# Expert rows: gathered and summed at the end, or scaled and added into the residual in DRAM as they are made

## The chip, the cores and the metric

One core of one Trainium2 chip runs the whole program. The metric is device time in microseconds for one execution, taken as a median of unprofiled runs: 1065.59 us for the kernel before (three runs, 1063.46 to 1066.72). A separate, profiled execution gives the trace.

## The reference

A two-layer decoder trunk over 512 tokens of width 1024, in float32. Layer 0 is latent attention and a dense SwiGLU; layer 1 is a pooling mixer and a routed mixture of experts; a last RMSNorm follows. What matters here is the end of layer 1:

```python
hn = rms_norm(h, ffn_norm[1])
# each token: its top 2 of 8 experts by hn @ router, gates = softmax of the two logits
y[token] = gate0 * expert0(hn[token]) + gate1 * expert1(hn[token])
# expert(x) = (silu(x @ w_gate) * (x @ w_up)) @ w_down, inner width 1344
h = h + y
out = rms_norm(h, final_norm)
```

## The kernel before

The tokens sit in `h`, four tiles (t = 0 to 3) of 128 tokens by 1024. After the router, the 1024 (token, expert) pairs are sorted into *jobs*, each one expert and a block of rows; job j owns rows j*144 on of two DRAM buffers, `xbuf` (normed inputs) and `ybuf` (expert outputs). GpSimd scatters the normed tokens into `xbuf` with eight indirect DMAs (L738; the row numbers are `dest`). With this input there are two *wide* jobs (144 rows, plain float32 matmuls, L1594 and L1618), then five *narrow* jobs in a loop and a *final* narrow job (128 rows). `before_last`, `narrow` and the expert of each job are read from a table at run time.

A narrow job needs its expert's 16.5 MB of weights. SP loads them as 18 units u0 to u17 of about 1 MB (two DMAs each, u17 half as large) into nine raw buffers (`RAWS`); it issues unit u when the unit nine earlier has been used (`n_used`). ScalarE rounds each unit to its high part (`unit_hi`, L1062), VectorE subtracts for the low part (`unit_lo`, L2250), and TensorE multiplies three times (L1190 to L1192). Units 0 to 7 and 10 to 13 are gate and up columns; `silu(f)`, `product(f)` (L2321), `turn(f)` (transposes, L1698), `act_hi_out(f)` (L1128) and `act_lo_out(f)` (L2326) bring activation group f to the down projection, which is `down_pair` over u8, u9, u14 to u17. `down_pair(1, 0)` (u14) waits for `act_lo_out(1)`. ScalarE's order near the end of a job is u13, u14, u15, `act_hi_out(1)`, u16, u17, `silu(2)`. VectorE's is u12, u13, u14, `act_lo_out(1)`, u15, u16, u17, `product(2)`.

At the end of a wide or a looped narrow job ScalarE and VectorE each copy one half of the job's output out of PSUM (L1103 and L2282; L1164 and L2372), and GpSimd stores it to `ybuf` (L753, L763, L775), waits for the landing and frees the buffer. GpSimd also loads the next job's rows from `xbuf` (L743, L749, L760, L772).

The final job's output is never stored. The tokens in it, and enough others to fill 128, are called *slots*. While the final job runs, GpSimd gathers, two per tile, the rows of `ybuf` that belong to tiles 0 to 2 (L782, `y_rows`), then three tiles for the slots (L791: their residual from `hbuf` and up to two rows of `ybuf`), and, once tile 0 is summed, the two of tile 3. VectorE adds them with their gates (`add_y`, L2302, two instructions per tile, put between the `unit_lo` of u12 to u15; `add_slots`, L2312). ScalarE squares (L1172) and VectorE scales (L2383) each tile after the final job's own work, SP stores the four tiles. Last, the slots' rows take the final job's PSUM (L2392), are normed (L1176 to L2398) and scattered over the output once the four stores have landed (L798).

`hbuf` holds a copy of the residual, stored by SP (`keep_h`) before the first job. During the dense feed-forward, GpSimd writes zeros to all of `xbuf` (L723) and to the rows of `ybuf` that no job may write (L727, L730).

Of the kernel before, what the change touches and what calls it, by code (L numbers as in the profile page):

```python
# [24 lines left out]
F32 = mybir.dt.float32  # L25
# [7 lines left out]
P = 128  # L33
# [34 lines left out]
YPIECES = 2 * (FI - 2)  # L68
YZERO = -(-(JMAX - E) * C // YPIECES)
# [84 lines left out]
def trunk(nc, a, out):  # L154
    plan = plan_weights()
    with ExitStack() as ctx:
# [49 lines left out]
        from_y = sb("from_y", [P, 2 * T], I32)  # L206
        gate_y = sb("gate_y", [P, 2 * T])
        spare_b = sb("spare_b", [P, T], BF16)
        slot_vals = sb("slot_vals", [P, T, 8])
        slot_info = sb("slot_info", [P, 8])  # L210
        slot_at = sb("slot_at", [P, 4], I32)
# [72 lines left out]
        y_in = view(0, 6 * D, 6)  # L284
        slot_h, slot_a, slot_b = (view((6 + n) * D, D) for n in range(3))
        slot_y = y_in[:, 2, :]
        n_x = view(4096, D)

# [34 lines left out]
        ybuf = nc.dram_tensor("ybuf", (JMAX * C, D), F32, kind="Internal").ap()  # L323
        hbuf = nc.dram_tensor("hbuf", (S, D), F32, kind="Internal").ap()
# [17 lines left out]
        y_gathered = [sem(f"y_gathered{t}") for t in range(T)]  # L342
# [114 lines left out]
        h_final = sem("h_final")  # L457
# [181 lines left out]
        def _(pool):  # L639
# [13 lines left out]
            for m in (ident, ident_b):  # L653
# [13 lines left out]
            g.iota(slot_vals[:, :, :], [[P, T], [0, 8]], base=0, channel_multiplier=1, allow_small_or_imprecise_dtypes=True  # L667
                   ).then_inc(iotas_ready, 1)
            g.iota(iota_j[:, :], [[1, NJ]], base=0, channel_multiplier=0, allow_small_or_imprecise_dtypes=True
                   ).then_inc(iotas_ready, 1)  # L670

# [44 lines left out]
            for i in range(FI):  # L716
                for j in range(FG):
                    if j == 0:
                        pool.wait_ge(prod_ready, i * FG + 2)
                    elif j == 2 and i < FI - 1:  # L720
                        pool.wait_ge(h_ffn, i * 8 + 4)
                    at = (i * FG + j) * XZERO
                    pool.dma_start(xbuf[at:at + XZERO, :], zero_rows[0:XZERO, :]).then_inc(zero_stored, 16)  # L723
                if i < E - 1:
                    at = (i + 1) * C + P if i else (E - 1) * C
                    rows = min(C - P if i else P, JMAX * C - YPIECES * YZERO - at)
                    pool.dma_start(ybuf[at:at + rows, :], zero_rows[0:rows, :]).then_inc(zero_stored, 16)  # L727
                for n in range(2 * i, min(2 * i + 2, YPIECES)):
                    at = JMAX * C - (n + 1) * YZERO
                    pool.dma_start(ybuf[at:at + YZERO, :], zero_rows[0:YZERO, :]).then_inc(zero_stored, 16)  # L730
# [5 lines left out]
            pool.wait_ge(zero_stored, 16 * (FI * FG + YPIECES + E - 1))  # L736
# [3 lines left out]
            pool.wait_ge(scattered, 16 * 2 * T)  # L740
            pool.sem_inc(yn_free, 1)
            pool.wait_ge(xT_done, 1)
            pool.dma_start(xg, xbuf[C:2 * C, :].rearrange("(k p) n -> p k n", p=CH)).then_inc(xg_landed, 16)  # L743
            pool.wait_ge(routed, 1)
            before_last = pool.value_load(table[0:1, NJ + 3:NJ + 4], min_val=1, max_val=JMAX - 1)
            with pool.Fori(0, before_last) as job:
# [3 lines left out]
                               ).then_inc(xg_landed, 16)  # L750
                pool.wait_ge(y_ready, job + 2)
                pool.wait_ge(y_ready_dve, job + 2)
                pool.dma_start(ybuf[bass.ds(job * C, C), :].rearrange("(k p) n -> p k n", p=CH), yn  # L753
                               ).then_inc(y_stored, 16)
                pool.wait_ge(xg_landed, job * 16 + 32)
                pool.wait_ge(y_stored, job * 16 + 16)
# [6 lines left out]
            pool.dma_start(ybuf[bass.ds(before_last * C, C), :].rearrange("(k p) n -> p k n", p=CH), yn  # L763
                           ).then_inc(y_stored, 16)
            pool.wait_ge(y_stored, before_last * 16 + 16)
            pool.sem_inc(n_y_free, 1)
            narrow = pool.value_load(table[0:1, NJ + 2:NJ + 3], min_val=1, max_val=JMAX)
            with pool.Fori(0, narrow) as n:

                pool.wait_ge(n_x_turned, n + 1)  # L770
                job = job_of(n + before_last + 1)
                pool.dma_start(n_x, xbuf[bass.ds(job * C + 2 * C, P), :]).then_inc(n_x_landed, 16)  # L772
                pool.wait_ge(n_y_left, n + 2)
                pool.wait_ge(n_y_right, n + 2)
                pool.dma_start(ybuf[bass.ds(job * C, P), :], n_y[:, :]).then_inc(n_y_stored, 16)  # L775
                pool.wait_ge(n_x_landed, n * 16 + 32)
                pool.wait_ge(n_y_stored, n * 16 + 16)
                pool.sem_inc(n_y_free, 1)

            def y_rows(t):  # L780
                for k in range(2):
                    pool.indirect_dma_start(out=y_in[:, (2 * t + k) % 6, :], out_offset=None, in_=ybuf,  # L782
                                            in_offset=bass.IndirectOffsetOnAxis(ap=from_y[:, k * T + t:k * T + t + 1], axis=0)
                                            ).then_inc(y_gathered[t], 16)

            pool.wait_ge(slots_known, 1)
            pool.wait_ge(h_stored, 16 * T)
            for t in range(T - 1):
                y_rows(t)
            for n, (dst, src) in enumerate(((slot_h, hbuf), (slot_a, ybuf), (slot_b, ybuf))):  # L790
                pool.indirect_dma_start(out=dst, out_offset=None, in_=src,  # L791
                                        in_offset=bass.IndirectOffsetOnAxis(ap=slot_at[:, n:n + 1], axis=0)
                                        ).then_inc(slot_landed, 16)
            pool.wait_ge(h_final, 1)
            y_rows(T - 1)
# [7 lines left out]
        def _(act):  # L803
# [224 lines left out]
            act.wait_ge(zero_stored, 16 * (FI * FG + YPIECES + E - 1))  # L1028
# [35 lines left out]
            def expert_job(job, final=False):  # L1064
# [37 lines left out]
                for b in range(2):  # L1102
                    last = s.copy(yn[:, 0, b * 512:b * 512 + 512], bank[4 + b][0:CH, :])  # L1103
# [12 lines left out]
            def narrow_job(n, final=False):  # L1116
# [24 lines left out]
                silu(1)  # L1141
                for u in (13, 14, 15):
                    unit_hi(u, n)
# [3 lines left out]
                if final:  # L1147
                    silu(2)
                    s.activation(warm[:, 0:1], eps_t[:, 0:1], ACT.Sqrt)
                    act_hi_out(2)  # L1150
                    return
# [12 lines left out]
                s.copy(n_y[:, 0:512], bank[4][:, :]).then_inc(n_y_left, 1)  # L1164
# [4 lines left out]

            for t in range(T):  # L1170
                act.wait_ge(h_final, t + 1)
                link(s.activation(n_y[:, :], h[:, t, :], ACT.Square, scale=D ** -0.5, accum_out=sumsq[:, t:t + 1]))  # L1172
                s.activation(rms[:, t:t + 1], sumsq[:, t:t + 1], ACT.Sqrt, bias=eps_t[:, 0:1]).then_inc(std_ready, 1)
# [11 lines left out]
        def _(pe):  # L1185
# [452 lines left out]
            def expert_job(job, final=False):  # L1638
# [16 lines left out]
                else:  # L1655
                    pe.wait_ge(slots_ready, 1)
                    for t in range(T):
                        last = t_.matmul(bank[2][:, 0:6], slot_of[:, t, :], slot_vals[:, t, 0:6], start=t == 0, stop=t == T - 1)
# [98 lines left out]
        def _(dve):  # L1757
# [388 lines left out]
            link(v.tensor_tensor(gate1[:, :], gate1[:, :], gate0[:, :], ALU.mult))  # L2146

# [42 lines left out]
            rel, in_last, out_last, near = (field(2 * n, 2) for n in range(4))  # L2190
            any_last, spare, slot, other = (field(8 + n) for n in range(4))
            at_last, own, moved, bound = (field(12 + n) for n in range(4))
            base_of, top_of, full = bound[:, 0:1], bound[:, 1:2], bound[:, 2:3]
# [227 lines left out]
```

## Time and profile before

| | us |
|---|---|
| median of three unprofiled runs | 1065.59 |
| the profiled execution | 1071.8 |
| its span (first to last instruction) | 1070.1 |
| TensorE busy in the span | 1017.4 |
| VectorE / ScalarE / GpSimd busy | 601.2 / 453.8 / 73.1 |

The mean granted TensorE clock is 0.983 of full speed. 226.55 MB move by DMA, 212 GB/s over the span. In the page's strip of 40 slices, TensorE is at 9 tenths or more in almost all but the last two (6 and 3), and the DMA engines are at 9 tenths in the ten slices before the last two. To read it: a busy engine is only a bound where nobody else makes it wait, and the average over the span says little about one stage. The stages that matter here are routing (604 to 620 us), the wide jobs (621 to 761), the narrow loop (761 to 994), the final job (994 to 1058) and the tail behind it.

### The profile page before, as it was taken

The numbers are of one execution on the slowest core, as the hardware profiler recorded it, in microseconds if no ns is written. First come the engines' busy times: TensorE is split into PE (matmuls) and PEld (weight loads), VectorE is DVE, ScalarE is ACT, GpSimd is POOL, SyncE is SP. The second block draws the span as 40 slices with busy tenths as digits, with TensorE's granted clock in tenths as the row PEclk, the third lists the DMA queues.
The fourth block names the chain that finished last, engine by engine and source line by source line (L and its number), as shares of the span: only waits on it lengthen the run. The fifth ranks groups of instructions, "written<-read, shape, count | busy, mean of one in ns | idle before, by whom it ended". The sixth has DMA issues, their size and how long they took to land.

```text
span 1070.1 us, 15078 instructions
## 1 busy us (share of the span) xinstructions
PE 1017.4 (95%) x5506; PEld 873.6 (82%) x5506; DVE 601.2 (56%) x816; ACT 453.8 (42%) x603; POOL 73.1 (7%) x138
## 2 busy tenths in 40 slices
PE   5999999999999999999999789999999999999963
PEld 5887887788888888888889679999887888888852
DVE  6575666354443434343457630100788989889875
ACT  5535554244232222223144200101777777777633
POOL 2200000000010100000000030000000000000330
PEclk9999999999999999999999899999999999999986
DMA  8021322535373736445327576895999999999982
GB/s 281 2 79 41 128 69 81 136 100 160 130 202 97 218 103 195 137 135 156 100 78 256 197 243 195 270 335 184 372 356 389 364 392 368 368 389 366 391 310 98
DMA packets 150155, 226.55 MB, mean 212 GB/s; under 512 B 16676, under 2 KB 97572, under 8 KB 150112
## 3 DMA queue, kind: packets, MB, share of 16 engines
q1 hardware_dynamic: 138464, 187.98, 52.6%
q0 software_dynamic: 10832, 37.44, 10.0%
q8 instruction: 28, 0.46, 0.2%
q10 hardware_dynamic: 816, 0.54, 0.2%
q14 instruction: 15, 0.12, 0.0%
HBM read 196.92 MB, written 29.02 MB: 211 GB/s over the span
## 4 chain that ended last, share of the span: by engine, by line
PE 86%; DVE 6%; DMA 3%; ACT 2%; issue 2%; SPq 0%; POOLq 0%; DVEq 0%; ACTq 0%
PE bank L1190 22%; PE bank L1191 22%; PE bank L1192 22%; PE bank L1594 8%; PE bank L1618 4%; DMA u_raw<-in_moe_w_down 2%; PE bank L1362 1%; PE bank L1202 1%; PE bank L1573 1%; PE bank L1342 1%; PE bank L1353 1%; PE bank L1499 1%; DVE w_lo L1771 1%; DVE u_lo L2250 1%; PE bank L1698 1%
## 5 line engine op out<-in xcount | busy, mean ns | idle before, releaser
L2250 DVE TENSOR_TENSOR u_lo<-u_raw,u_hi 128x2048 fp32r<-128x2048 f32 (+1 forms) x108 | 217.6, 2046 | 12.2 <-ACT u_hi L1062 11.8
L1062 ACT CAST u_hi<-u_raw 128x2048 fp32r<-128x2048 f32 (+1 forms) x108 | 185.0, 1723 | 73.9 <-DMA u_raw<-in_moe_w_up 37.5
L1190 PE MATMUL bank<-big_hi,w_lo 128*128 128x512 f32 (+2 forms) x352 | 134.4, 382 | 0.0
L1192 PE MATMUL bank<-big_hi,w_hi 128*128 128x512 f32 (+2 forms) x352 | 134.3, 381 | 0.0
L1191 PE MATMUL bank<-big_lo,w_hi 128*128 128x512 f32 (+2 forms) x352 | 134.2, 381 | 0.0
L1771 DVE TENSOR_TENSOR w_lo<-stage_own,w_hi 128x1024 fp32r<-128x1024 f32 (+1 forms) x89 | 103.3, 1207 | 13.8 <-ACT w_hi L817 13.8
L1190 PE MATMUL bank<-u_hi,nx_lo 128*128 128x512 f32 (+1 forms) x288 | 106.5, 370 | 0.0
L1004 ACT ACTIVATE scratch<-bank 128x512 f32<-128x512 f32 x21 | 12.6, 598 | 218.8 <-PE bank L1192 218.8
L1192 PE MATMUL bank<-u_hi,nx_hi 128*128 128x512 f32 (+1 forms) x288 | 104.5, 363 | 0.0
L1191 PE MATMUL bank<-u_lo,nx_hi 128*128 128x512 f32 (+1 forms) x288 | 104.5, 363 | 0.0
L2028 DVE TENSOR_TENSOR scratch<-scratch,bank 128x512 f32<-128x512 f32 x21 | 14.5, 688 | 151.6 <-ACT scratch L1004 151.6
L817 ACT CAST w_hi<-stage_own 128x1024 fp32r<-128x1024 f32 (+1 forms) x89 | 87.0, 1036 | 10.6 <-DMA stage_own<-in_mla_w_uq 5.6
L1594 PE MATMUL bank<-scratch,u_raw 128*128 128x144 f32 x640 | 84.4, 290 | 4.6 <-issue 3.1
L1594 PEld LDWEIGHTS bank<-scratch,u_raw 128*128 128x128 f32 x640 | 81.6, 193 | 5.5 <-issue 3.7
L1190 PE MATMUL bank<-w_hi,act_lo_mem 128*128 128x512 f32 (+1 forms) x216 | 81.5, 377 | 0.6 <-DVE act_lo_mem L1831 0.6
L1191 PE MATMUL bank<-w_lo,act_hi_mem 128*128 128x512 f32 (+1 forms) x216 | 80.7, 373 | 0.0
L1192 PE MATMUL bank<-w_hi,act_hi_mem 128*128 128x512 f32 (+1 forms) x216 | 80.6, 373 | 0.0
L1190 PEld LDWEIGHTS bank<-big_hi,w_lo 128*128 128x128 f32 x352 | 66.1, 188 | 12.8 <-issue 0.2
L1192 PEld LDWEIGHTS bank<-big_hi,w_hi 128*128 128x128 f32 x352 | 66.1, 188 | 12.4
L1191 PEld LDWEIGHTS bank<-big_lo,w_hi 128*128 128x128 f32 x352 | 66.1, 188 | 12.4
L1190 PE MATMUL bank<-u_hi,na_lo 128*128 128x512 f32 (+1 forms) x132 | 55.3, 419 | 8.2 <-DVE na_lo L2326 7.3
L2256 DVE TENSOR_TENSOR qr_now<-krT,bank 128x144 f32<-128x144 f32 x20 | 6.1, 304 | 99.6 <-ACT krT L1070 99.0
(342 smaller groups left out, 1746.9 us busy)
## 6 DMA issues: line engine op xcount, KB each, us to landing
u_raw<-in_moe_w_gate SPq DMA_DIRECT2D x68, 512.0 KB, 6.8
u_raw<-in_moe_w_up SPq DMA_DIRECT2D x68, 512.0 KB, 8.1
u_raw<-in_moe_w_down SPq DMA_DIRECT2D x64, 512.0 KB, 9.5
stage_own<-in_ffn_w_gate SPq DMA_DIRECT2D x21, 512.0 KB, 6.0
stage_own<-in_ffn_w_up SPq DMA_DIRECT2D x21, 512.0 KB, 7.2
stage_own<-in_ffn_w_down SPq DMA_DIRECT2D x21, 512.0 KB, 4.4
xbuf<-scratch POOLq DMA_DIRECT2D x21, 496.0 KB, 5.9
u_raw<-in_moe_w_down SPq DMA_DIRECT2D x8, 1024.0 KB, 7.8
```

What stands on the lines that cost most here:

```text
L817: s.copy(w_hi[0:parts, sl, 0:n], stage(st)[0:parts, 0:n]).then_inc(weight_hi, 1)
L1004: s.activation(f_silu[:, j % 2, :], bank[2 * (j % 2)][:, :], ACT.Silu).then_inc(silu_ready, 1)
L1062: s.copy(u_hi[u % HIS][0:rows, 0:size], u_raw[u % RAWS][0:rows, 0:size]).then_inc(n_hi, 1)
L1190: t_.matmul(dst, st_lo, mv_hi, start=start, stop=False, skip_group_check=check)
L1191: t_.matmul(dst, st_hi, mv_lo, start=False, stop=False, skip_group_check=check)
L1192: return t_.matmul(dst, st_hi, mv_hi, start=False, stop=stop, skip_group_check=check)
L1202: last = t_.transpose(bank[banks[k // 4]][:, k % 4 * P:k % 4 * P + P], src[:, k * P:(k + 1) * P], ident[:, :])
L1594: last = t_.matmul(dst[:, 0:C], u_raw[u % RAWS][:, at:at + P], xT[:, k, :], start=k == 0, stop=k == KD - 1)
L1618: last = t_.matmul(bank[4 + k // 3][:, col:col + C], u_raw[u % RAWS][0:parts, at:at + P], e_act[0:parts, f % 2, :], start=f == 0 and k % 3 ...
L1771: v.tensor_tensor(w_lo[0:parts, sl, 0:n], stage(st)[0:parts, 0:n], w_hi[0:parts, sl, 0:n], ALU.subtract).then_inc(weight_lo, 1)
L2028: v.tensor_tensor(f_act[:, j % 2, :], f_silu[:, j % 2, :], bank[2 * (j % 2) + 1][:, :], ALU.mult).then_inc(prod_ready, 1)
L2250: v.tensor_tensor(u_lo[u % RAWS][0:rows, 0:size], u_raw[u % RAWS][0:rows, 0:size], u_hi[u % HIS][0:rows, 0:size], ALU.subtract).then_inc(n ...
```

## The change

Each job's output row is multiplied by its gate while it leaves PSUM, and the GpSimd DMA that stored it is replaced by an indirect DMA that adds it to its token's row of `hbuf`. For this a small DRAM table `info` holds, per job row, the token number and the gate. It is filled by two strided DMAs with "no token" entries (rows 512 to 655 of `hbuf`, gate zero) and by eight indirect DMAs of 8 bytes per row after those to `xbuf`. Before each addition GpSimd loads the job's part of the table and waits for it. At the end, one gather brings the slots' rows from `hbuf` and four plain loads bring `h` back; ScalarE squares the tiles within the final job.

```diff
+            for c in range(2 * T):
+                pool.indirect_dma_start(out=info, out_offset=bass.IndirectOffsetOnAxis(ap=dest[:, c:c + 1], axis=0),
+                                        in_=token_gate[:, c, :], in_offset=None).then_inc(scattered, 16)
...
             with pool.Fori(0, narrow) as n:
-                pool.wait_ge(n_x_turned, n + 1)
+                pool.wait_ge(n_x_hi, n + 2)
                 pool.dma_start(n_x, xbuf[...]).then_inc(n_x_landed, 16)
+                pool.wait_ge(final_landed, 16)
                 pool.wait_ge(n_y_left, n + 2)
                 pool.wait_ge(n_y_right, n + 2)
-                pool.dma_start(ybuf[bass.ds(job * C, P), :], n_y[:, :]).then_inc(n_y_stored, 16)
+                pool.indirect_dma_start(out=hbuf, out_offset=bass.IndirectOffsetOnAxis(ap=n_info[:, 0:1], axis=0),
+                                        in_=n_y[:, :], in_offset=None, compute_op=ALU.add).then_inc(n_y_stored, 16)
                 pool.wait_ge(n_x_landed, n * 16 + 32)
                 pool.wait_ge(n_y_stored, n * 16 + 16)
+                pool.dma_start(n_info[:, :], info[bass.ds(job * C + C, P), :]).then_inc(n_info_landed, 16)
+                pool.wait_ge(n_info_landed, n * 16 + 32)
                 pool.sem_inc(n_y_free, 1)
...
             pool.wait_ge(slots_known, 1)
-            pool.wait_ge(h_stored, 16 * T)
-            for t in range(T - 1):
-                y_rows(t)
-            for n, (dst, src) in enumerate(((slot_h, hbuf), (slot_a, ybuf), (slot_b, ybuf))):
-                pool.indirect_dma_start(out=dst, ...)
-            pool.wait_ge(h_final, 1)
-            y_rows(T - 1)
+            pool.indirect_dma_start(out=slot_h, out_offset=None, in_=hbuf, ...).then_inc(slot_landed, 16)
+            for t in range(T):
+                pool.dma_start(h[:, t, :], hbuf[t * P:(t + 1) * P, :]).then_inc(h_back, 16)
```

On ScalarE, in the final job, and the scaled copies (VectorE's halves likewise, `tensor_scalar` in place of `tensor_copy`):

```diff
-                    last = s.copy(yn[:, 0, ...], bank[4 + b][0:CH, :])
+                    last = s.activation(yn[:, 0, ...], bank[4 + b][0:CH, :], ACT.Copy, scale=yn_gate[:, 0, :])
...
+                def square(t):
+                    act.wait_ge(h_back, 16 * T)
+                    link(s.activation(n_y[:, :], h[:, t, :], ACT.Square, scale=D ** -0.5, accum_out=sumsq[:, t:t + 1]))
+
+                if final:
+                    for t, u in enumerate((13, 14, 15)):
+                        unit_hi(u, n)
+                        square(t)
+                    act_hi_out(1)
+                    square(3)
+                    unit_hi(16, n)
+                    unit_hi(17, n)
+                    silu(2)
+                    s.activation(rms[:, 0:T], sumsq[:, 0:T], ACT.Sqrt, bias=eps_t[:, 0:1]).then_inc(std_ready, 1)
+                    act_hi_out(2)
+                    return
```

VectorE loses `add_y` and `add_slots`, and most of the small routing instructions of L2217 to L2233, and gains two 128x4 copies into `token_gate` after L2146. The slots' sum takes one value of the matmul of `slot_of` in place of three. `ybuf` and its zeros are gone; two stores of zeros to `hbuf` rows 512 to 655 and the two strided stores to `info` take their place. The same narrow-loop pattern holds in the wide jobs, where the addition is two indirect DMAs of 72 rows.

## Rows read from the trace of the kernel before

**Rows 1.** The page, section 4: shares of the chain that ended last.

```profile
PE 86%; DVE 6%; DMA 3%; ACT 2%; issue 2%; SPq 0%; POOLq 0%; DVEq 0%; ACTq 0%
```

**Rows 2.** Windows: one narrow job, the final job's first 46.5 us, the rest.

```profile
core 0: us, PE busy (x) PEld busy (x) DVE busy (x) ACT busy (x) POOL busy (x), PEclk, DMA share, GB/s
949.40:995.90 46.50, 46.50 (x230) 39.13 (x229) 41.14 (x29) 34.84 (x29) 1.07 (x2) 1.00 1.03 378
995.90:1042.40 46.50, 39.21 (x182) 32.81 (x180) 35.43 (x25) 23.34 (x19) 18.30 (x12) 0.90 0.95 353
1042.40:1070.10 27.70, 10.12 (x33) 7.58 (x33) 16.83 (x22) 10.09 (x23) 0.99 (x1) 0.68 0.24 95
```

**Rows 3.** Windows of 5 us in the final job, the same columns.

```profile
1020.00:1025.00 5.00, 5.00 (x32) 4.64 (x31) 4.56 (x5) 1.64 (x2) 2.74 (x2) 1.00 1.03 409
1025.00:1030.00 5.00, 4.63 (x32) 4.36 (x30) 3.89 (x4) 1.58 (x1) 2.90 (x2) 1.00 1.02 407
1030.00:1035.00 5.00, 0.00 (x0) 0.00 (x0) 2.29 (x1) 1.66 (x2) 0.00 (x0) 0.77 1.05 347
1035.00:1040.00 5.00, 3.10 (x7) 2.51 (x8) 3.88 (x4) 1.05 (x2) 0.00 (x0) 0.50 0.74 220
1040.00:1045.00 5.00, 2.39 (x6) 1.34 (x4) 4.96 (x4) 4.66 (x5) 0.00 (x0) 0.71 0.00 1
```

**Rows 4.** Timeline of PE: start, length, line; final job's first, gated and last instructions.

```profile
994.19 0.50 PE L1190 MATMUL bank<-u_hi,nx_lo 128*128 128x512 f32 x1
...
1036.90 0.79 PE L1190 MATMUL bank<-u_hi,na_lo 128*128 128x512 f32 x1 [7.28 <-DVE na_lo L2326]
...
1047.78 0.69 PE L1698 MATMUL bank<-ident,na_nat 128*128 128x128 f32 x2 [5.39 <-DVE na_nat L2321]
...
1057.51 0.39 PE L1192 MATMUL bank<-u_hi,na_hi 64*128 64x512 f32 x1
```

**Rows 5.** Timeline of ACT: u14, u15, act_hi_out(1) and a square, final job.

```profile
1028.42 1.91 ACT L1062 CAST u_hi<-u_raw 128x2048 fp32r<-128x2048 f32 x1 [3.90 <-DMA u_raw<-in_moe_w_down]
1033.67 1.90 ACT L1062 CAST u_hi<-u_raw 128x2048 fp32r<-128x2048 f32 x1 [3.34 <-DMA u_raw<-in_moe_w_down]
1035.47 0.58 ACT L1128 CAST na_hi<-bank 128x512 fp32r<-128x512 f32 x1
...
1049.15 1.06 ACT L1172 ACTIVATE n_y<-h 128x1024 f32<-128x1024 f32 x1
```

**Rows 6.** Groups of instructions by line: the sums removed and the scatter before routing ends.

```profile
L2302 DVE SCALAR_TENSOR_TENSOR h<-scratch,gate_y,h 128x1024 f32<-128x1024 f32 x8 | 10.2, 1281 | 0.1
L2312 DVE SCALAR_TENSOR_TENSOR scratch<-scratch,slot_info 128x1024 f32<-128x1024 f32 x2 | 2.6, 1278 | 0.0
...
L738 POOL DMA_INDIRECT xbuf<-scratch,dest x8 | 7.8, 976 | 42.6 <-DVE dest L2172 40.5 <-issue 2.1
```

**Rows 7.** Timelines of a looped narrow job: VectorE's u8 and u9, TensorE's u8.

```profile
916.20 4.48 DVE L2250 TENSOR_TENSOR u_lo<-u_raw,u_hi 128x2048 fp32r<-128x2048 f32 x2
...
923.47 0.39 PE L1190 MATMUL bank<-u_hi,na_lo 128*128 128x512 f32 x1
```

**Rows 8.** Timeline of POOL: an input load, the last store, first and ninth gather.

```profile
688.08 0.71 POOL L749 DMA_DIRECT2D scratch<-xbuf  x1 [56.40 <-PE bank L1584]
...
997.48 0.54 POOL L775 DMA_DIRECT2D ybuf<-n_y  x1 [15.79 <-DVE n_y L2372]
1006.02 2.95 POOL L782 DMA_INDIRECT scratch<-ybuf,from_y  x1 [8.01 <-issue]
...
1021.52 1.80 POOL L791 DMA_INDIRECT scratch<-ybuf,slot_at  x1 [0.30 <-issue]
```

**Rows 9.** Issue to landing: by DMA group (last figure, us), and the ninth gather alone.

```profile
ybuf<-n_y POOLq DMA_DIRECT2D x5, 512.0 KB, 7.0
...
posi<-in_positions ACTq DMA_DIRECT2D x1, 2.0 KB, 4.5
...
DMA to landing us min/median/max: 16.4/16.4/16.4
```

More of the change, by code:

```diff
@@ L341, in trunk @@
         y_stored = sem("y_stored")
-        y_gathered = [sem(f"y_gathered{t}") for t in range(T)]
+        info_landed = sem("info_landed")
+        n_info_landed = sem("n_info_landed")
+        h_back = sem("h_back")
         out_stored = sem("out_stored")
@@ L723, in _ @@
                     pool.dma_start(xbuf[at:at + XZERO, :], zero_rows[0:XZERO, :]).then_inc(zero_stored, 16)
[L724 to L730, printed above, removed]
+                if i < 2:
+                    at = S + i * CH
+                    pool.dma_start(hbuf[at:at + CH, :], zero_rows[0:CH, :]).then_inc(zero_stored, 16)
+                elif i == 2:
+                    for k in range(2):
+                        pool.dma_start(info.rearrange("(j k p) n -> k p j n", k=2, p=CH)[k],
+                                       no_token[:, k:k + 1, :].broadcast_to([CH, JMAX + 2, 2]), allow_slow_non_contiguous=True
+                                       ).then_inc(zero_stored, 16)
             pool.wait_ge(xn_ready, 3 * T)
@@ L1146, in narrow_job @@
                     unit_hi(u, n)
[L1147 to L1151, printed above, removed]
                 unit_hi(18, n)
@@ L2188, in field @@
                 return late[:, n * T:(n + width) * T]
[L2190 to L2193, printed above, removed]
+            rel, in_last = field(0, 2), field(2, 2)
+            any_last, spare, slot, other, at_last, bound = (field(4 + n) for n in range(6))
+            base_of, full = bound[:, 0:1], bound[:, 1:2]
             first_in, second_in = in_last[:, 0:T], in_last[:, T:2 * T]
-            first_out, second_out = out_last[:, 0:T], out_last[:, T:2 * T]
             link(v.scalar_tensor_tensor(base_of, ends[:, E - 1:E], 2.0, ends[:, 2 * E - 1:], ALU.add, ALU.max))
@@ L2342, in narrow_job @@
                 product(1)
-                if final:
-                    for t in range(T):
-                        unit_lo(12 + t, n)
-                        if t == 2:
-                            act_lo_out(1)
-                        add_y(t)
-                    unit_lo(16, n)
-                    unit_lo(17, n)
-                    product(2)
-                    add_slots()
-                    act_lo_out(2)
-                    return
                 for u in (12, 13, 14):
@@ L2360, in narrow_job @@
                 product(2)
+                if final:
+                    act_lo_out(2)
+                    return
                 dve.wait_ge(n_x_hi, n + 2)
```

136 lines of the change are left out of this document (56 added, 80 removed).

## The prediction, made before the changed kernel was run

> **What bounds the kernel now.** Read three views in this order. The chain of work that ended last is 86% TensorE [rows 1], so what counts is where TensorE is *not* at work. The windows show two regimes [rows 2]. In a looped narrow job TensorE is busy for all 46.5 us at full clock, while DMA runs at 378 GB/s: TensorE is the bound, DMA close behind. In the final job it is busy only 39.2 of the first 46.5 us, and 10 of the 27.7 behind them. By its timeline the final job starts at 994.2 and its last matmul ends at 1057.9 [rows 4]. Unstalled it would take a looped job's 46.5 us less 0.9 us (eight transposes for a next job that isn't there), and end at 1039.8. So 18.1 us are lost there, and that is all that the change can win on TensorE.
>
> Where they go: TensorE stops for 7.3 us before 1036.9, waiting for act_lo_out(1) [rows 4], which stands behind ScalarE's u14 and u15, each held by its weights (3.9 and 3.3 us of waiting) [rows 5]. The weights are late because 11 gathers of 0.52 MB each (5.8 MB) share the DMA engines: these are saturated at 400 to 409 GB/s until 1030 and then empty out until 1040 [rows 3]. TensorE resumes at half clock (granted 0.50), stops again for 5.4 us for product(2), which stands behind VectorE's late units and add_y, and is slow again [rows 3, 4].
>
> **The change, part by part.** The sum is made against the profiled execution (span 1070.1, 1071.8 with what lies around it), which is 6.2 us above the median of the runs; I carry the difference in us over to the median.
>
> *Routing.* Two 128x4 copies on VectorE and eight more scatters on GpSimd. One scatter is 0.98 us and 0.3 us of issue [rows 6], so 8 x 1.28 = 10.2 us in GpSimd's queue, and behind them a wait for landing and a small load, then xg. The xg that matters to the next use waits for TensorE anyway, 56.4 us in the one row shown [rows 8]. Zero. If that cover were gone, it would be about 20 us once. The removed zeros of ybuf and the strided info stores lie beside the dense layers, where TensorE is at 9 tenths: zero, within 1 us either way.
>
> *Copies with a gate.* Same sizes, same engines, off the path. Zero; at most 0.1 us per job.
>
> *The add in place of the store, five narrow jobs.* No row shows an adding DMA. It moves at least the store's 0.52 MB and reads as much again. The room: engines under backlog move about 405 GB/s [rows 3], a job needs 378 [rows 2], so (405 - 378) x 46.5 us = 1.3 MB per job. If the add costs x stores' worth of DMA time, the extra is (x - 1) x 0.52 MB; below x = 3.4 it fits. A burst that delays a unit is hidden as well: u8's low part is done at 918.4 and TensorE takes it at 923.5 [rows 7], 5.0 us of slack. I take x = 2 and zero cost; the bounds are a plain store (x = 1) and x = 6. The Trainium skill, "Collectives: The Full Stack", section on the bandwidth ceiling, says a DMA add is slower because it needs two source reads on one ring, about half the rate. By that x is 2 and this term is zero; no trace of before shows it.
>
> *The new waits on GpSimd.* Behind the add stand a load of info, a wait, and n_y_free. In the loop n_y_free is wanted a whole job later: zero. In the last iteration they delay the final loads, below.
>
> *The final job.* Removed: 11 gathers (5.8 MB), VectorE's ten sums, 12.8 us [rows 6]. Added: one gather and four loads, 2.6 MB. New order: after u13 ScalarE waits for *all four* tiles of h, and u14, u15 and act_hi_out(1) queue behind that wait; TensorE's u14 to u17 wait for these. So the question is when h is back; call it A.
>
> GpSimd: the add is issued at 997.5 as the store was [rows 8]. Landing: a store takes 7.0 us, the slowest gather 16.4 [rows 9]; I take 10, nearer the store, since GpSimd's queue holds nothing else. Info load: 4.5 us for 2 KB, 7.0 for a store [rows 9]; I take 4.5. From the old store's landing (1004.5) to the first gather (1006.0) were 1.5 us of issue [rows 8]. So the first of the five transfers is issued at 997.5 + 10 + 4.5 + 1.5 = 1013.5. Rate: the ninth gather landed at 1021.5 + 16.4 = 1037.9, nine issued since 1006.0, so 4.7 MB in 31.9 us, 148 GB/s, for GpSimd's stream beside SP's. 2.6 MB at 150 take 17.5 us: A = 1031.0. The other way round, from bytes: 3.1 MB fewer and 0.5 MB more for the add is 2.6 MB off the end of the backlog, that is all of 1035 to 1040 (1.1 MB) and most of 1030 to 1035 (1.7 MB) [rows 3], so everything lands by 1031. The two agree.
>
> From A: three squares at 1.2 (1.06 and a read-out) [rows 5], u14 and u15 at 1.9, give 7.4; act_hi_out(1) to TensorE's start took 1.4 (1035.5 to 1036.9) [rows 4, 5]: TensorE resumes at A + 8.8 = 1039.8, 2.9 us *later* than before. But what follows is closer: VectorE has no sums left, so u15, u16 and u17 (2.2 each for the first two [rows 7], half that for u17) and product(2) put turn(2) at A + 15.0 = 1046.0, against 1047.8. From there to the end took 10.1 us [rows 4], mostly at half clock. This time TensorE has only about a 1 us gap before turn(2); the granted clock had risen again by 1040 to 1045 after the work of 1036.9 to 1042 [rows 3]. I take full clock, 10.1 less 2.5 = 7.6: end at A + 22.6 = 1053.6 against 1057.9, **4.3 us** gained. The final norm's four scalings, after A + 17, take 5 us and are done before that; the tail behind TensorE (12.2 us) stays. 1065.59 - 4.3 = **1061.3**. The break-even is A = 1035.3, and each us of A is one us of time.
>
> Bounds: add and info at 7.0 and 4.5, A = 1028.0 at the gathers' rate, 1023.6 at 200 GB/s: 1053.9. Add 16.4 and info 7.0: start at 1022.4, A = 1032 if SP's weights are through by then (0.4 MB per us alone), 1039.9 if not: 1070.2.
>
> **The rivals.**
> *A fair split.* GpSimd's stream gets half of 400 GB/s: 13.1 us, A = 1026.6, time 1056.9. For it: SP's backlog is smaller, having had 8 us alone. Against: 148 measured. The Trainium skill, "DMA: Bandwidth & Descriptors", section on queues and rings, says each engine goes round-robin by packet between the rows with work; taken as equal shares this is that case, and the 148 GB/s against SP's 250 or so disagree.
>
> *Nothing gained.* The wait for h takes the place of the wait for weights almost exactly, A about 1034 to 1036, or half clock stays to the end (2.5 us): 1064 to 1066.
>
> *h comes back late, slower.* Place: ScalarE's wait after u13. From A over 1035.3. The add's landing and the info load stretch under 405 GB/s of weights to 16 and 7 us and the five transfers stay at 150 GB/s: A = 1040, 1070. For it: gathers under this load needed up to 16.4 us; five transfers, all needed, wait on three round trips. Against: late transfers find SP finished.
>
> *The add is heavy, slower.* x over 3.4. At x = 6 the five jobs exceed their room by 1.3 MB each, 3.3 us, 16 in all less 5 of slack, and A moves 6 us back: about 1079. For it: DMA is at 378 of 405. The half rate of the skill speaks against.
>
> **How the numbers follow.** Forecast 0.40 (own range 1058 to 1064); fair split or earlier 0.20; nothing gained 0.18; h late 0.14; heavy add 0.08. A measurement can tell about 0.3%, 3.2 us, from no change, so faster is below 1062.4: three quarters of the forecast and the fair split, 0.50; within 0.28; slower 0.22. The range 1053 to 1070 takes in the bounds of A, and leaves out the heavy add and the ends of two others.
>
> **What would show it.** Right: looped jobs still 46.5 us with TensorE full; ten fewer sums; four loads of h issued from about 1015, landed near 1031; ScalarE idle some 10 us before the first square, with that DMA as its releaser; TensorE resuming at about 1040, turn(2) at 1046. Wrong: TensorE idle in the loop (heavy add); u14 waiting for its own weights rather than for h; h landed before 1024 or after 1036; a table load between the silus.

## The result, and the profile after

The changed kernel is slower: 1071.57 us median of four runs (1069.06 to 1074.74) against 1064.76 (1063.46 to 1066.72), ratio 1.0065, 95% interval 1.0046 to 1.0084. The forecast was 1061.3, faster. On two other chips it is slower still: 1.0165 (1.0143 to 1.0187) on one, 1.0163 (1.0143 to 1.0184) on another.

The page's chain of work that ended last [rows 1]:

```profile
PE 78%; DMA 8%; DVE 6%; issue 3%; ACT 3%; SPq 0%; POOL 0%; POOLq 0%; ACTq 0%; DVEq 0%
```

TensorE's share fell from 86% to 78% and DMA's rose from 3% to 8%: the chain now runs through transfers. Windows of the changed kernel: a looped narrow job, and three stretches of 5 us in the final job (columns as in [rows 2]):

```profile
907.28:955.67 48.39, 46.89 (x230) 39.08 (x229) 41.42 (x29) 34.98 (x29) 3.94 (x3) 1.00 1.04 362
...
1035.00:1040.00 5.00, 0.08 (x1) 0.00 (x0) 0.00 (x0) 1.34 (x3) 0.00 (x0) 0.83 0.30 114
1040.00:1045.00 5.00, 0.00 (x0) 0.00 (x0) 2.29 (x1) 4.89 (x5) 0.00 (x0) 0.50 0.00 0
1045.00:1050.00 5.00, 2.72 (x6) 2.15 (x7) 3.38 (x3) 4.86 (x7) 0.00 (x0) 0.50 0.00 0
```

A looped job takes 48.4 us instead of 46.5, TensorE is idle 1.5 us of it, and DMA, at a share of 1.04, moves *less* per us (362 GB/s for 378). GpSimd's timeline, the second load of xg, two additions, and what brings h back:

```profile
682.59 0.70 POOL L767 DMA_DIRECT2D scratch<-xbuf  x1 [39.19 <-PE bank L1606]
...
955.67 2.85 POOL L798 DMA_INDIRECT hbuf<-n_y,n_info  x1 [10.97 <-ACT n_y L1191]
...
1003.08 2.88 POOL L798 DMA_INDIRECT hbuf<-n_y,n_info  x1 [10.92 <-ACT n_y L1191]
1014.64 0.57 POOL L802 DMA_DIRECT2D n_info<-info  x1 [8.68 <-DMA hbuf<-n_y,n_info]
1020.82 1.62 POOL L807 DMA_INDIRECT scratch<-hbuf,slot_at  x1 [5.61 <-DMA n_info<-info]
1022.42 2.19 POOL L810 DMA_DIRECT2D h<-hbuf  x4
```

Four marks on this timeline cut every kernel of this study into stages that can be compared: the second xg load (it waits for TensorE in the first wide job), the last wide xg load (65.9 us later in all of them), the last store or addition, the scatter to `out`.

| kernel | second xg load at | last wide xg load to last store or add | from there to the scatter to out | span |
|---|---|---|---|---|
| before | 688.1 | 243.5 | 64.8 | 1070.1 |
| after | 682.6 | 254.6 | 62.3 | 1073.0 |

So the profiled execution lost 11.1 us in the narrow stage and won 2.5 in the final job and 5.5 in the start, which is 3.1 in all for 2.9 us of span. The medians of the runs differ by 6.8 (this profile of the kernel before, 1071.8 us, lies above all its four runs in the comparison). That start is the odd part: it is in no other profile of the changed kernel (experiments, below).

### The profile page after: what moved, and what is told of

It reads as the page before. It is cut to its first block, busy times and chain, and to the rows that moved or that the text cites. A ratio compares the mean times of both kernels' runs of the same rounds, so it can differ in the third digit from the quotient of the medians.

```text
span 1073.0 us, 15043 instructions
## 1 busy us (share of the span) xinstructions
PE 1014.1 (95%) x5506; PEld 870.5 (81%) x5506; DVE 588.7 (55%) x791; ACT 453.6 (42%) x599; POOL 92.5 (9%) x140
## 4 chain that ended last, share of the span: by engine, by line
PE 78%; DMA 8%; DVE 6%; issue 3%; ACT 3%; SPq 0%; POOL 0%; POOLq 0%; ACTq 0%; DVEq 0%
PE bank L1212 20%; PE bank L1214 19%; PE bank L1213 19%; PE bank L1616 7%; DMA u_raw<-in_moe_w_up 4%; PE bank L1640 4%; PE bank L1384 1%; DMA h<-hbuf 1%; PE bank L1595 1%; DMA hbuf<-n_y,n_info 1%; PE bank L1224 1%; PE bank L1364 1%; PE bank L1375 1%; PE bank L1521 1%; DVE w_lo L1793 1%
## 5 line engine op out<-in xcount | busy, mean ns | idle before, releaser
L1616 PE MATMUL bank<-scratch,u_raw 128*128 128x144 f32 x640 | 81.7, 286 | 1.3 <-DVE scratch L2232 1.3
L1212 PE MATMUL bank<-u_hi,na_lo 128*128 128x512 f32 (+1 forms) x132 | 54.3, 411 | 18.0 <-DVE na_lo L2318 12.2
L1212 PE MATMUL bank<-w_hi,big_lo 128*128 128x512 f32 (+2 forms) x160 | 59.0, 369 | 2.8 <-DVE big_lo L1813 2.7
```

What stands on the lines that cost most here:

```text
L1212: t_.matmul(dst, st_lo, mv_hi, start=start, stop=False, skip_group_check=check)
L1616: last = t_.matmul(dst[:, 0:C], u_raw[u % RAWS][:, at:at + P], xT[:, k, :], start=k == 0, stop=k == KD - 1)
```

## Experiments

The same marks in the kernels that follow. *Pitch* is the time from one looped job's store or addition to the next. e1 to e4, e5 to e8, e9 to e12 and the last three each shared a chip:

| kernel | second xg load at | narrow stage | final | span | ratio to before (95%) |
|---|---|---|---|---|---|
| e1 no add | 697.8 | 244.3 | 61.5 | 1077.3 | 1.0061 (1.0039 to 1.0082) |
| e2 no info load | 697.6 | 251.4 | 57.0 | 1079.2 | one run |
| e3 before, one more load | 687.4 | 246.6 | 68.1 | 1076.3 | 1.0049 (1.0031 to 1.0067) |
| e4 squares last | 695.8 | 252.2 | 53.9 | 1075.5 | 1.0072 (1.0051 to 1.0093) |
| e5 changed kernel | 697.2 | 252.1 | 62.9 | 1085.7 | 1.0165 (1.0143 to 1.0187) |
| e6 info scatters later | 688.3 | 252.9 | 63.1 | 1077.9 | 1.0074 (1.0057 to 1.0091) |
| e7 before, eight more scatters | 696.7 | 244.1 | 64.2 | 1079.4 | 1.0107 (1.0090 to 1.0124) |
| e8 e6 and squares last, by tile | 686.2 | 254.7 | 51.9 | 1066.3 | 1.0001 (0.9986 to 1.0015) |
| e9 e8, all scatters later | 685.0 | 253.6 | 52.8 | 1064.9 | 0.9977 (0.9966 to 0.9989) |
| e10 before, scatters later | 683.8 | 244.6 | 63.8 | 1065.9 | 0.9972 (0.9961 to 0.9983) |
| e11 before, one more store | 686.8 | 247.8 | 64.4 | 1073.2 | 1.0055 (1.0033 to 1.0077) |
| e12 half of the add | 696.4 | 246.5 | 61.0 | 1077.6 | one run |
| e13 changed kernel again | 696.1 | 254.3 | 63.1 | 1087.0 | 1.0163 (1.0143 to 1.0184) |
| e14 e10 again | 683.7 | 244.3 | 64.4 | 1066.1 | 0.9972 (0.9962 to 0.9983) |
| e15 kernel before | 688.1 | 243.7 | 64.6 | 1070.1 | one run |

**e1_no_add.** The changed kernel, its additions turned into plain indirect writes (in the wide jobs likewise), so the residual and the other expert's row are lost.

```diff
-    in_=n_y[:, :], in_offset=None, compute_op=ALU.add).then_inc(n_y_stored, 16)
+    in_=n_y[:, :], in_offset=None).then_inc(n_y_stored, 16)
```

> The changed kernel with the addition left out of its indirect DMAs: they write the scaled rows over those of hbuf (so the residual and the other expert's row are lost from the sum), everything else stays. Theory 1 (the DMA addition itself lengthens the looped narrow jobs, by the second read and the dependent write): the pitch of the looped jobs falls from 47.4 to 49.0 us back to 46.5 to 46.8, the weights' waits on ScalarE shrink to those of before, and the time falls by 9 to 11 us to 1061 to 1063. Theory 2 (what costs is around the addition: the indirect form with its 2.8 us on GpSimd, the table load, the later load of inputs): the pitch stays at 48 or more and the time at 1070 to 1072.

Measured: the looped job is back at 46.5 us (five writes issued from 821.84 to 1007.95, four pitches), so the addition itself, not the indirect form, the table load or the waits, makes the loop long. What the DMA engines were occupied with over four jobs (queue: packets, MB, share of 16 engines), e1 from 822 to 1008 us:

```profile
q1 hardware_dynamic: 32211, 66.11, 97.4%
q0 software_dynamic: 1280, 4.20, 5.7%
```

and the changed kernel (e5) from 824 to 1015 us:

```profile
q1 hardware_dynamic: 31939, 65.57, 95.7%
q0 software_dynamic: 1280, 4.20, 8.4%
```

q0 is GpSimd's queue. The same 4.20 MB take 5.7% of 186 us, 10.6 us, as four loads and four writes, 1.33 us each; with additions they take 8.4% of 191, 16.0 us. An addition occupies the engines for 1.33 + 5.4 / 4 = 2.7 us, twice the write. My x = 2 was right, and so, in this trace, is the half rate that the Trainium skill gives in "Collectives: The Full Stack", section on the bandwidth ceiling. But both lines of e1 sum to 103%, as [rows 2] had it: there was little free engine time for the 1.35 us more. The total, 1078.4 us, missed what was expected of it (1061 to 1063), because its start was late, by 9.7 us against the kernel before and by 15.2 against the first profile. That was new, and e5 to e7 look into it.

**e2_no_info.** The changed kernel without the load of the table in the loop (the gates and rows of the first narrow job are used for all, so a load and a wait per job are left out).

```diff
-    pool.dma_start(n_info[:, :], info[bass.ds(job * C + C, P), :]).then_inc(n_info_landed, 16)
-    pool.wait_ge(n_info_landed, n * 16 + 32)
```

> The changed kernel without the per-job load of the table in the narrow loop: all five jobs add by the list of the first (rows land on wrong tokens). Theory 1 (the addition): the pitch of the looped jobs stays at 47.4 to 49.0 us. Theory 2 (the many 8-byte rows of the table load cost DMA time): it falls by 1 us or more. Both: the final loads are issued 6 us earlier relative to the job's start, since the 5.2 us of the table load are gone from the chain, so TensorE's gap before u14 shrinks by about 6 us from 10.

Measured: pitch 48.0 us (822.96 to 1014.82 in four), so the table load costs the loop nothing. It does cost the final job: 57.0 us against 62 to 63, as h is asked for 6 us earlier (TensorE's gap before u14 is 7.0 us instead of 12.2).

**e3_more_load, e11_more_store.** The kernel before with one more plain transfer of 0.5 MB per looped job, once a load (e3), once a store (e11). GpSimd also waits for its landing before it goes on, which the lines below leave out.

```diff
     pool.dma_start(ybuf[bass.ds(job * C, P), :], n_y[:, :]).then_inc(n_y_stored, 16)
+    pool.dma_start(zero_rows, xbuf[bass.ds(job * C + 2 * C, P), :]).then_inc(more_landed, 16)   # e3
+    pool.dma_start(more[:, :], n_y[:, :]).then_inc(more_stored, 16)                             # e11
```

> The kernel before with one more plain 0.5 MB load per looped narrow job, issued by GpSimd right behind the store; nobody uses what it brings. Theory F (the DMA engines had no room in the loop, whatever the byte rate says: their share is 1.03 there): each looped job grows by 0.52 MB / 378 GB/s = 1.4 us, less what the slack takes up once: pitch 47.5 to 47.9, time 1070 to 1071. Theory H (there was room for 1 MB per job, as the prediction said, and the addition is worth four or more stores): pitch 46.5, TensorE without a gap, time within 1 us of before.

> The kernel before with one further plain store of n_y (0.5 MB, to a buffer that nobody reads) in each looped narrow job, behind its own. A further load of that size took the job from 46.5 to 47.15 us; the addition, which by the trace occupies the DMA engines as long as store and load together, takes it to 47.9 to 48.4. Theory Q (only occupied engine time counts): 47.1 to 47.2. Theory W (what writes costs more than what reads): 47.6 to 48.4. Total by Q 1.003 to 1.005, by W 1.006 to 1.010.

**e12_half_add.** The changed kernel, adding only the first 64 rows of each looped job (the others are left out).

```diff
-    out=hbuf, out_offset=bass.IndirectOffsetOnAxis(ap=n_info[:, 0:1], axis=0),
-    in_=n_y[:, :], in_offset=None, compute_op=ALU.add).then_inc(n_y_stored, 16)
+    out=hbuf, out_offset=bass.IndirectOffsetOnAxis(ap=n_info[0:64, 0:1], axis=0),
+    in_=n_y[0:64, :], in_offset=None, compute_op=ALU.add).then_inc(n_y_stored, 16)
```

> The changed kernel in which a looped narrow job adds only its first 64 rows (the other 64 are left out, so the time is that of less work). Engine time of half an addition is that of the plain store. Theory Q (engine time alone): pitch 46.5 to 46.6. Theory H (the adding form costs more than its engine time): 47.1 to 47.6. The start as in the changed kernel, second xg load at 695 to 698.

Measured, mean of four pitches: before 46.53, half an addition 46.57, one more load 47.16, one more store 47.34, a whole addition 47.8 (e5), 48.4 (first profile) and 48.7 (e13). Half an addition takes 1.6 us of engine time by its own rows (6.1% of 192 us against e1's 10.6), little more than a plain write's 1.33, and costs nothing, as theory Q had it. 1.3 us more of engine time cost 0.6 us as a load and 0.8 as a store. So e3 lies between its two theories (H 46.5, F 47.5 to 47.9), and e11 between Q (to 47.2) and W (from 47.6): the loop had room for about half of what was added, and the engines' share rose from 102.8% in the kernel before to 104.6% in e3. e3's final job is 3.3 us longer too, which is why its total (1.0049) grew by more than its pitches. A whole addition has the engine time of a store and a load and costs 0.4 to 1.4 us more than e11. Why isn't settled. To add at another point of the job, where it might collide less, wasn't tried.

How the cost reaches TensorE, by ScalarE's waits in the loop of the changed kernel, 811 to 1003 us (total, times, longest):

```profile
ACT u_hi L1077 <- DMA u_raw<-in_moe_w_down: 28.9, 20, 2.5
ACT u_hi L1077 <- DMA u_raw<-in_moe_w_up: 22.1, 30, 2.1
```

and of the kernel before, 811 to 997 us:

```profile
ACT u_hi L1062 <- DMA u_raw<-in_moe_w_up: 20.8, 25, 1.7
ACT u_hi L1062 <- PE bank L1192: 13.3, 15, 1.1
...
ACT u_hi L1062 <- DMA u_raw<-in_moe_w_down: 4.9, 4, 1.7
```

Before, 13.3 us of ScalarE's waiting were for TensorE: it was ahead. After, it waits for weights almost alone, 51 us against 26, and VectorE and TensorE behind it. TensorE's own waits in the same stretch, of which the kernel before shows none:

```profile
PE bank L1212 <- DVE na_lo L2323: 4.6, 4, 1.3
PE bank L1720 <- DVE na_nat L2313: 1.6, 3, 0.8
```

**e4_squares_last.** The changed kernel with ScalarE's squares, and so its wait for h, behind all of the final job's work.

```diff
-    for t, u in enumerate((13, 14, 15)):
-        unit_hi(u, n)
-        square(t)
+    for u in (13, 14, 15):
+        unit_hi(u, n)
     act_hi_out(1)
-    square(3)
...
     act_hi_out(2)
+    for t in range(T):
+        square(t)
+    s.activation(rms[:, 0:T], sumsq[:, 0:T], ACT.Sqrt, ...)
```

> The changed kernel with the four squares of ScalarE and their wait for h moved from between u13 and u17 of the final job to behind act_hi_out(2), as before; the same result. Theory A (the wait for h in ScalarE's queue holds u14 to u17, nothing else does): no gap of TensorE before u14, its last matmul at about 1046 to 1048 instead of 1061, then squares, norm and stores bring the time 8 to 10 us down, to 1061 to 1064. Rival (the final job's weights are late anyway, because the five transfers share the engines): u14 or u15 waits for its weights until 1035 or later, TensorE ends after 1052 and the time is within 3 us of the changed kernel.

Measured: 53.9 us from the last addition to the scatter to out, against 62 to 63: 8 to 9 us won. TensorE's gap before u14 is gone, and its last matmul ends 47.7 us after the last addition instead of 57.9. The wait for h was the end's bound. The total (1078.2 us, ratio 1.0072, where 1061 to 1064 was expected) doesn't show it, as the second xg load is 13.2 us later than in the first profile.

**e5_changed, e6_info_later, e7_more_scatters.** Second xg load at 695.8 to 697.8 in every variant with the eight scatters to info in their place. The changed kernel itself (e5); the same with those scatters behind a wait for eight `expert_used` (e6); the kernel before with eight more, idle ones (e7).

```diff
+    pool.wait_ge(expert_used, AHEAD + 8)     # e6: behind the xg load, ahead of the scatters to info
     for c in range(2 * T):
         pool.indirect_dma_start(out=info, out_offset=..., in_=token_gate[:, c, :], ...).then_inc(scattered, 16)
```

```diff
+    for c in range(2 * T):                   # e7, behind the kernel's own eight
+        pool.indirect_dma_start(out=more, out_offset=..., in_=dest[:, 0:2], ...).then_inc(scattered, 16)
```

> The changed kernel once more, beside the runs below. In the profile of the kernel before the second xg load is issued at 688.1 us; in the changed kernel's first profile at 682.6, in three variants of it at 695.8 to 697.8. Theory S (the eight further scatters hold up the other engines at the start of the wide jobs in most executions): this profile too shows that load at 695 to 698, and TensorE busy under 30 of the 40 us from 620 to 640 plus 600 to 620; ratio to the kernel before 1.006 to 1.011 on this chip. Rival N (the first profile is the changed kernel's usual start, the variants differ by chance): the load at 682 to 688.

> The changed kernel with the eight scatters to info (and the load behind them) put behind the first xg load and a wait for eight expert_used, some 25 us into the first wide job. Theory S: TensorE, VectorE and ScalarE are free from about 629 us, as in the kernel before (its eight scatters end at 626), the second xg load is issued at 685 to 689, and the total is 8 to 10 us under the changed kernel's on this chip, if the later scatters hold nobody up while the engines are in their loops. Rival L (any run of indirect scatters holds the engines wherever it stands): a stall of some 10 us moves with them to about 650 and nothing is gained. Rival N: start and total as in the changed kernel, within 2 us.

> The kernel before with eight further indirect scatters of 8 bytes per row, to a DRAM buffer that nobody reads, behind its own eight. Theory S: the stall in its start ends at about 639 instead of 629 us, the second xg load moves from 688 to 696 to 698, and the total grows by 8 to 10 us (ratio 1.008 to 1.010). Rival N (the scatters are covered, as I predicted at price zero): ratio within 0.998 to 1.002. Rival K (code loading or the loop's entry stalls the engines, not the scatters): start as in the kernel before.

Windows 620 to 640 us of e5 and of e7 (each has its last scatter at about 635):

```profile
620.00:640.00 20.00, 8.88 (x55) 8.15 (x54) 4.17 (x17) 0.63 (x2) 13.77 (x15) 0.81 0.47 167
```

```profile
620.00:640.00 20.00, 8.95 (x40) 8.07 (x41) 5.88 (x31) 0.29 (x1) 12.61 (x14) 0.69 0.44 163
```

TensorE works 9 of 20 us. Its timeline in e5, and ScalarE's first product of the wide job:

```profile
630.89 0.28 PE L1616 MATMUL bank<-scratch,u_raw 128*128 128x144 f32 x1 [0.21 <-issue]
633.00 0.28 PE L1616 MATMUL bank<-scratch,u_raw 128*128 128x144 f32 x1 [1.83 <-issue]
634.42 0.28 PE L1616 MATMUL bank<-scratch,u_raw 128*128 128x144 f32 x1 [1.13 <-issue]
636.55 0.40 PE L1616 MATMUL bank<-scratch,u_raw 128*128 128x144 f32 x1 [1.85 <-issue]
638.64 3.76 PE L1616 MATMUL bank<-scratch,u_raw 128*128 128x144 f32 x15 [1.70 <-issue]
...
638.96 0.29 ACT L1085 ACTIVATE krT<-bank 128x144 f32<-128x144 f32 x1 [18.61 <-remote]
```

Single matmuls with 1 to 2 us between them, with "issue" as the cause (waiting for nothing that the profile shows), until GpSimd's scatters are through. ScalarE's first product comes at 638.96; in the first profile of the same kernel it comes at 625.96, 13.0 us earlier. "Remote" is a releaser that the profile can't name. It isn't DMA bandwidth: in that stretch the queues are nearly empty (e5, 628 to 638 us, all that moved):

```profile
q0 software_dynamic: 351, 0.33, 10.5%
```

No load of instructions (the page's queue q8) is among it either; the next one comes after 652 us. Nor is it the first xg load, which stands behind the scatters: it is issued at 638.1 in e5 and at 642.7 in the first profile, which has no stall.

e5's own ratio, 1.0165, is above the 1.006 to 1.011 that was expected of it. e7 confirms the scatters as the cause in the kernel before: load at 696.65 instead of 688, 10.8 us in the total (8 to 10 expected). e6 takes them away from that place: 688.3, and 9.9 us less than e5 in the medians (1078.08 against 1087.97 on one chip). Its window, 640 to 665 us, has the scatters beside the wide job:

```profile
640.00:665.00 25.00, 24.01 (x193) 23.44 (x192) 1.21 (x4) 0.98 (x5) 8.50 (x9) 1.00 0.80 215
```

Eight scatters cost TensorE 1.0 us there (the kernel before has 25.00 in this window) and 9 us while the engines enter the wide job. Rival L is out.

**e8_later_and_last, e9_all_later, e10_before_later.** e8: e6, with e4's order and a square root and a scaling for each tile. e9: e8 with the scatters to xbuf behind the same wait. e10: the kernel before, one line:

```diff
+    pool.wait_ge(expert_used, AHEAD + 8)
     for c in range(2 * T):
         pool.indirect_dma_start(out=xbuf, out_offset=..., in_=xn[:, c % T, :], in_offset=None).then_inc(scattered, 16)
```

```diff
     for t in range(T):                       # e8, ScalarE
         square(t)
+        s.activation(rms[:, t:t + 1], sumsq[:, t:t + 1], ACT.Sqrt, bias=eps_t[:, 0:1]).then_inc(std_ready, 1)
```

> The changed kernel with the scatters to info put later (as in the run above), ScalarE's squares behind act_hi_out(2) and a square root and a scaling for each tile, so that the scalings are done before the slots' sum. Sum of the parts, if theory S holds: 8 to 10 us less at the start, 8 in the final job (from job start to the last scatter 65.6 to 57.4 us in the run with the squares last), 2.5 from the scalings: 17 to 21 us under the changed kernel; against the kernel before 0.988 to 0.992, although the narrow loop still pays about 11 us for the additions. If rival L holds: 0.997 to 1.001.

> The version with the later info scatters, late squares and scalings by tile, and now the eight scatters to xbuf too behind the wait for eight expert_used. Theory S (scatters hold the engines only while these enter the wide job, not later): TensorE runs through 620 to 640 us, the second xg load is issued at 680 to 683 instead of 686 to 688, total 4 to 6 us under the version before it, 0.993 to 0.996 of the kernel before. Rival L (the stall goes where the scatters go): 1.000, within 0.002, with TensorE stalled between 640 and 665.

> The kernel before with its own eight scatters behind a wait for eight expert_used, nothing else changed. In its profile the second xg load was issued at 688.1 and TensorE worked 15.4 of the 20 us from 620 to 640. Theory S: load at 682 to 684, ratio 0.994 to 0.996. Rival L or no stall by scatters at all: 0.998 to 1.002.

Measured: e8 is 17.3 us under e5 (1070.67 against 1087.97), inside 17 to 21; against the kernel before 1.0001 where 0.988 to 0.992 stood, since I had worked that out from a changed kernel at 1.007, not at 1.0165. In e8 the last scaling is over before the slots' sum begins (VectorE, start, length):

```profile
1052.07 1.28 DVE L2369 SCALAR_TENSOR_TENSOR h<-h,rms,gain_last 128x1024 f32<-128x1024 f32 x1
1054.36 1.41 DVE L2376 SCALAR_TENSOR_TENSOR scratch<-bank,slot_info,scratch 128x512 f32<-128x512 f32 x2 [1.00 <-PE bank L1217]
```

e10's window from 620 to 640 and its load:

```profile
620.00:640.00 20.00, 18.68 (x164) 18.59 (x163) 6.24 (x33) 0.87 (x3) 1.09 (x2) 1.00 0.41 114
...
683.79 0.71 POOL L750 DMA_DIRECT2D scratch<-xbuf  x1 [23.71 <-PE bank L1585]
```

TensorE is busy 18.7 of 20 us for the 15.4 of the kernel before. On their chip e10 (1067.40 us) and e9 (1067.78) beat the kernel before (1069.89), by less than was expected: e10 by 2.5 us where 4 to 6 stood, e9 by 2.1 where it was 4 to 7 (its load, expected at 680 to 683, is at 685.0). In e9, which has eight scatters from 637.6 and eight from 658.7 on, TensorE works only 24.1 of the 25 us to 665 and 23.4 of the next 25: these aren't quite free.

**e13_changed_again, e14_later_again, e15_before_itself.** The changed kernel, e10 and the kernel before, unedited, profiled on one further chip.

> The changed kernel once more, on a chip of its own choosing, beside a profile of the kernel before on the same chip. Its ratio was 1.0065 in the first comparison, whose profile shows the second xg load at 682.6 us, and 1.0165 in another, whose profile shows it at 697.2. Theory C (the stall by the scatters is there on some chips or executions and not on others, and explains the difference of the two ratios): load at 682 to 684 goes with a ratio of 1.005 to 1.008, load at 695 to 698 with 1.015 to 1.018. Rival D (the difference is elsewhere): the two don't go together.

> The kernel before, unchanged, for a profile beside the other two on the same chip. Theory C: where the changed kernel has no stall, this has none either, and its second xg load is issued near 683 instead of 688; where the changed kernel has one, 687 to 688.

> The kernel before with its scatters behind eight expert_used, once more. Theory C: ratio 0.996 to 0.998 on a chip on which the kernel before stalls, 0.999 to 1.001 on one on which it doesn't; load at 683 to 684 in either case.

Second xg load of e13 and of e15:

```profile
696.09 0.70 POOL L767 DMA_DIRECT2D scratch<-xbuf  x1 [57.34 <-PE bank L1606]
```

```profile
688.09 0.71 POOL L749 DMA_DIRECT2D scratch<-xbuf  x1 [55.16 <-PE bank L1584]
```

The sum closes on this pair: 8.0 us at the start, 10.6 in the narrow stage, -1.5 in the final job, 17.1 for 16.9 us of span and 17.7 in the medians. For the changed kernel, loads at 696 to 697 go with ratios of 1.016, the one at 682.6 with 1.0065, as theory C has it; e14 repeats e10's 0.9972, with its load at 683.7. That the chip of the first comparison has no stall in either kernel would also explain why the kernel before runs at 1064.8 there and at 1069.9 to 1071.3 on four others, but I have no profile of it from that chip. This part is argued, not shown, and it doesn't close: without a stall on either side the stages give 11.1 - 2.5 = 8.6 us, where the medians differ by 6.8.

## Why the prediction was wrong

*The add in place of the store: the step that failed.* The cost of an addition (x = 2) was right to the tenth. Wrong was the room, (405 - 378) x 46.5 us = 1.3 MB. [rows 2] shows the DMA share of a looped job at 1.03; the 405 GB/s of [rows 3] stand at the same share in another mix of transfers, and a gap between two byte rates isn't idle engine time. Counted in engine time, the loop had room for about half of one more plain transfer (e3, e11), not for 1.3 MB, and TensorE was busy for all 46.5 us besides. Priced at zero, the additions cost 11.1 us in the first profile's narrow stage (8.5 and 10.6 in two others; e1, without them, is 0.8 over the kernel before), of which 7.4 (4 x 1.84) are four pitches and 3.7 the way from the last wide job to the first narrow addition. My rival of a heavy add named place and sign, but put its threshold at x = 3.4, where half an addition (x = 1.2) was free and a load or store more (x = 2) was not: it should have had the largest chance. The 5.0 us of slack at u8 [rows 7] may hide a burst once; it can't cover a cost that comes in every job.

*Routing: priced at zero, 8 to 10 us in every profile but the first.* The cover I named was true of GpSimd's own queue: its load of xg does wait 39 to 59 us for TensorE. But I looked only at who waits for those instructions. [rows 6] says when they run, and beside them the other engines enter the wide job. In the kernel before, TensorE already lost 4.6 us there (15.4 of 20 us; 1.3 in e10, without scatters there), and I hadn't asked why. This term isn't in the changed kernel's first profile, where the medians differ by 6.8 us; where it is, they differ by 17 to 18.

*Copies with a gate, the waits in the loop: zero,* right. e1 has both and its pitch is 46.5.

*The final job: right in mechanism, 1.8 us too good.* From the last addition to A, the moment h is back, I had 10 + 4.5 + 1.5 + 17.5 = 33.5 us. By GpSimd's and ScalarE's timelines:

```profile
1038.55 1.06 ACT L1160 ACTIVATE n_y<-h 128x1024 f32<-128x1024 f32 x1 [14.50 <-DMA h<-hbuf]
...
1045.84 0.59 ACT L1143 CAST na_hi<-bank 128x512 fp32r<-128x512 f32 x1
```

```profile
1047.28 0.79 PE L1212 MATMUL bank<-u_hi,na_lo 128*128 128x512 f32 x1 [12.20 <-DVE na_lo L2318]
...
1053.38 0.44 PE L1720 MATMUL bank<-ident,na_nat 128*128 128x128 f32 x2 [0.93 <-DVE na_nat L2313]
...
1060.61 0.39 PE L1214 MATMUL bank<-u_hi,na_hi 64*128 64x512 f32 x1
```

11.6 (addition, from its issue to the next), 6.2 (table load) and 17.7 (five transfers) make 35.5. That the addition took 11.6 where I had 10 isn't the adding: e1's last plain indirect write took 11.4 from its issue to the next. TensorE resumes at A + 8.7 (I had 8.8) and ends at A + 22.4 (22.6). From the last addition to TensorE's end are 57.9 us, before 60.4, forecast 56.1: 2.5 us won in place of 4.3, the missing 2 in A. The stream rate that I took from nine gathers, 148 GB/s, held for the five transfers too (2.6 MB in 17.7 us). The fair split fell, and with it the equal shares between queues that I had read into the Trainium skill's "DMA: Bandwidth & Descriptors", section on queues and rings. After 12.2 us without work TensorE ran at the lower of its levels (granted 0.50, 1.2 GHz) until 1050, as in [rows 3]. From turn(2) on I had taken the full level, and that held: turn(2) starts at A + 14.8 (I had 15.0) and the end comes 7.6 us later, as forecast. The windows behind 1050:

```profile
1050.00:1055.00 5.00, 4.08 (x16) 3.03 (x15) 3.80 (x5) 2.86 (x6) 0.00 (x0) 0.80 0.00 0
1055.00:1060.00 5.00, 5.00 (x23) 3.87 (x22) 4.96 (x6) 0.00 (x0) 0.00 (x0) 1.00 0.52 210
```

*What I had called a sign of a wrong forecast* did show: TensorE idle in the loop. All my rivals but one lay in the final job; the loop cost four times what the final job gave back.

## What to carry to other kernels

Take a loop's free DMA time from the share of occupied engine time, not from the distance between two byte rates: at a share of 1.03 a further 1.3 us of plain transfer cost this loop 0.6 to 0.8 us, whatever the GB/s said, and an adding DMA counts twice. When an edit adds instructions in the shadow of one queue, look at what every other engine is doing at that moment, above all where they enter new code; a run of indirect DMAs was better issued once they were at work. And a wait for data that only a final step needs goes behind the work that doesn't need it (8 to 9 us here).

## What the hardware showed that I hadn't expected

- Eight indirect scatters of 8 bytes per row, 10 us on GpSimd, held TensorE, ScalarE and VectorE up for 8 to 10 us while these entered the wide job, with the DMA engines nearly idle, and TensorE by 1.0 us once it was in it. The profile puts the gaps down to issue and to remote. What the engines share there stays open, as does why one profile (load at 682.6) has none of it.
- An adding DMA of 0.5 MB occupied the DMA engines for 2.7 us, a plain one for 1.33. Its late landing (10.3 us, the direct store 7.0) and its hold on GpSimd (2.85 us, the store 0.54) come with the indirect form, not with the adding: e1's plain indirect writes landed after 10.7 and kept GpSimd for 2.2 to 4.5, and the first one of the last wide job kept it for 11.1 us (9.5 with the addition). The changed kernel's DMA groups, and the last one in e1 (last figure, us from issue to landing):

```profile
h<-hbuf POOLq DMA_DIRECT2D x4, 512.0 KB, 12.4
...
n_info<-info POOLq DMA_DIRECT2D x6, 1.0 KB, 5.1
hbuf<-n_y,n_info POOLq DMA_INDIRECT x5, 10.3
```

```profile
hbuf<-n_y,n_info POOLq DMA_INDIRECT x5, 10.7
```

- Half an addition in place of the store is free (46.57 us a job, in one profile); the whole one, 1.35 us more of engine time than the store, costs 1.2 to 2.2 us a job, a plain load or store more 0.6 to 0.8.
